# Half slabs of the memory keys and values inside the steps of the forgetting attention, and its forget sums added on VectorE

## The reference, cut to what matters

```python
rq, rk, rv, rg, fq, fk, fv, ff = split(rmsnorm(x, g_mix) @ w_in)        # 8 + 8 heads of 64
ret = silu(rg) * head_group_norm(chunk_retention(rotary(rq), rotary(rk), rv), g_ret_out)
F = cumsum(log_sigmoid(ff + b_forget))                                    # per head and token
logits = q.k / 8 + F[query] - F[key], causal                              # forgetting attention
h = x + concat([ret, softmax(logits) @ fv]) @ w_out
kv = rmsnorm(mem, g_mem) @ w_xkv                                          # 256 memory tokens
k, v = split(kv);  k = rmsnorm(k per head of 256, g_xk)
h = h + cross_attention(rmsnorm(h, g_xattn) @ w_xq, k, v) @ w_xo
h = h + (silu(hn @ w_gate) * (hn @ w_up)) @ w_down                        # then the second block
```

## Time and profile before

| | us |
|---|---|
| median of 3 runs | 1389.61 (1389.35 to 1390.12) |
| the profiled execution, as timed | 1390.99 |
| its span in the profile | 1389.2 |
| retention on PE | 179.9 to 200.6 |
| forgetting attention on PE, first to last step | 201.4 to 253.1 |
| first matmul of "out" | 306.5 |

### The profile page before, as it was taken

How to read it: one execution, slowest core, us unless ns; L and a number is a source line. 1 busy time by engine, 2 the same in 40 slices (tenths; PEclk the granted TensorE clock), 3 DMA queues, 4 the chain that set the end, 5 groups by cost and what they waited for, 6 DMA issues and landing times.

```text
span 1389.2 us, 17280 instructions
## 1 busy us (share of the span) xinstructions
PE 1354.4 (97%) x6530; PEld 1089.1 (78%) x6530; DVE 664.3 (48%) x978; ACT 623.5 (45%) x867; POOL 613.6 (44%) x448
## 2 busy tenths in 40 slices
PE   8999999999999999999999999988999999999999
PEld 7877955888876888888888887854878888888887
DVE  5434948355452553434343317588256455554111
ACT  5555238544364443433432123688244545554211
POOL 3444320474520455556555544312336555555453
PEclk9999999999999999999999999999999999999999
DMA  7223220152220244444346432200312222323422
GB/s 269 92 91 106 75 99 24 61 182 91 91 77 15 91 152 150 146 148 146 136 144 265 173 130 106 92 31 31 122 61 91 91 98 95 108 91 136 182 92 91
DMA packets 29216, 155.23 MB, mean 112 GB/s; under 512 B 3057, under 2 KB 4465, under 8 KB 14961
## 3 DMA queue, kind: packets, MB, share of 16 engines
q1 hardware_dynamic: 29168, 154.57, 31.1%
HBM read 152.46 MB, written 2.10 MB: 111 GB/s over the span
## 4 chain that ended last, share of the span: by engine, by line
issue 39%; PE 30%; POOL 26%; DVE 4%; DMA 1%; POOLq 0%; SPq 0%; ACT 0%
POOL wlo L392 26%; PE lin L1400 10%; PE lin L1402 10%; PE lin L1401 10%; DVE small L1045 1%; DVE expd L1056 1%; DMA raw<-w_slabs 1%; PE lin L1628 0%; DVE xl L899 0%; DVE win L1277 0%; DVE small L1049 0%; POOLq L401 0%; DVE xl L923 0%; DVE tmp L905 0%; PE att L1465 0%
## 5 line engine op out<-in xcount | busy, mean ns | idle before, releaser
L392 POOL TENSOR_TENSOR wlo<-raw,whi 128x512 fp32r<-128x512 f32 x444 | 613.4, 1414 | 760.2 <-ACT whi L419 501.1
L1400 PE MATMUL lin<-xh,whi 128*128 128x512 f32 x1072 | 420.5, 392 | 5.4 <-POOL wlo L392 3.6
L1402 PE MATMUL lin<-xh,wlo 128*128 128x512 f32 x1072 | 417.4, 389 | 0.0
L1401 PE MATMUL lin<-xl,whi 128*128 128x512 f32 x1072 | 417.2, 389 | 0.0
L1400 PEld LDWEIGHTS lin<-xh,whi 128*128 128x128 f32 x1072 | 201.2, 188 | 55.4 <-issue 9.0
L419 ACT ACTIVATE whi<-raw 128x2048 fp32r<-128x2048 f32 x66 | 126.7, 1919 | 261.8 <-PE lin L1402 256.2
L1402 PEld LDWEIGHTS lin<-xh,wlo 128*128 128x128 f32 x1072 | 201.2, 188 | 42.4
L1401 PEld LDWEIGHTS lin<-xl,whi 128*128 128x128 f32 x1072 | 201.3, 188 | 41.3 <-issue 0.2
L1400 PE MATMUL lin<-fh,whi 128*128 128x512 f32 x352 | 137.0, 389 | 0.0
L1401 PE MATMUL lin<-fl,whi 128*128 128x512 f32 x352 | 136.9, 389 | 0.0
L1402 PE MATMUL lin<-fh,wlo 128*128 128x512 f32 x352 | 136.9, 389 | 0.0
(11 more groups left out here) (337 smaller groups left out, 1919.7 us busy)
## 6 DMA issues: line engine op xcount, KB each, us to landing
raw<-w_slabs SPq DMA_DIRECT2D x111, 1024.0 KB, 4.8
adar<-ada SPq DMA_DIRECT2D x48, 512.0 KB, 5.5
decay<-decay SPq DMA_DIRECT2D x4, 512.0 KB, 7.9
h<-x_t SPq DMA_DIRECT2D x3, 512.0 KB, 6.5
out_t<-h SPq DMA_DIRECT2D x3, 512.0 KB, 8.2
rope<-rope SPq DMA_DIRECT2D x2, 512.0 KB, 7.2
memx<-mem_t SPq DMA_DIRECT2D x1, 1024.0 KB, 5.6
adar<-c_row SPq DMA_DIRECT2D x2, 512.0 KB, 6.1
```

The costliest lines, as they stand in the source:

```text
L392: return nc.gpsimd.tensor_tensor(wlo[s][:, ks, :], raw[s][:, ks, :], f(whi[s][:, ks, :]), ALU.subtract)
L1400: nc.tensor.matmul(out, whi_, xhi_, start=first, stop=False)
L1401: nc.tensor.matmul(out, whi_, xlo_, start=False, stop=False)
L1402: return nc.tensor.matmul(out, wlo_, xhi_, start=False, stop=last)
```

## The change

- PE puts one half slab of the memory (24 matmuls of 256 columns) behind the transposes of each of the 16 steps: slabs 14 to 21 are done in steps 0 to 15. The stage between the attention and "out" is gone. "out" starts with the slab form that waits for each input tile (first_pair).
- ACT, in every odd step, takes the result of the slab out of PSUM and then makes whi of the slab after next (memory_out). So whi of slab 22, the first of "out", is made in step 13, and that of slab 23 in step 15.
- PE no longer adds F by selr.fstack in each step. It makes these products once per head, 512 columns wide, in retention (forget_sums); ACT copies them to SBUF (minus_sums), and DVE adds the scores to them and takes the minimum of the negated sums in one instruction (tensor_tensor_reduce), which also writes the sums back to PSUM. The exponential then has scale -1.
- Memory norm (memx load, squares, sums, hi and lo) and the first parts of the group norm move into retention; the reciprocals and products of the group norm move into steps 1 to 13 on DVE.
- Retention's banks are dealt out differently: blocks s = 0 and s = 3 share two banks, and block s = 1 shares its two with the forget sums.
- SP: memx comes before the decay tables of pairs 2 and 3; the tile of w_ada comes after slabs 22 to 25. The row c still comes after the wait for all scores and ahead of slab 22.
- In slabs 4 to 7 ACT makes whi between the copies of the two tiles and not behind both.
- Two unused numbers in the count of bank pairs are gone, and some tiles lie elsewhere in SBUF.

```diff
@@ SyncE @@
             load_pairs(1, SLAB0["memk"] // 2 + 1)
+            sp.wait_ge(slab_done, SLAB0["memk"])
+            sp.dma_start(memx[:, :, :], mem_t.rearrange("(k p) m -> p k m", p=P)).then_inc(tables_in, 16)
             for c in range(2, RET_HEADS // 2):
...
-            sp.wait_ge(ret["pv"], RET_HEADS // 2)
-            sp.dma_start(memx[:, :, :], mem_t.rearrange("(k p) m -> p k m", p=P)).then_inc(tables_in, 16)
...
             load_pairs(SLAB0["memk"] // 2 + 1, SLAB0["out"] // 2)
             sp.wait_ge(fox["scores"], 32)
             load_c()
+            load_pairs(SLAB0["out"] // 2, SLAB0["xq"] // 2)
+            sp.wait_ge(xkn["out"], 2 * X_HEADS)
             load_ada(0, 0)
-            load_pairs(SLAB0["out"] // 2, SLAB0["ffn"] // 2 + 2)
+            load_pairs(SLAB0["xq"] // 2, SLAB0["ffn"] // 2 + 2)
@@ ScalarE @@
                     last.then_inc(rope["copy"], 1)
-                make_hi(u + 2)
+                    if j == 0:
+                        make_hi(u + 2)
...
+            def forget_tiles(c):
+                for hh in range(2):
+                    act.wait_ge(ff["mm"], 1 + 2 * c + hh + 1)
+                    nc.scalar.activation(minus_sums[c][hh][:, :], att[2 + hh], ACT.Copy).then_inc(ff["minus"], 1)
...
+            def memory_out(u):
+                g = SLAB0["memk"] + u
+                act.wait_ge(slab_done, g + 1)
+                if 2 <= u <= 4:
+
+                    act.wait_ge(xkn["stat"], (u - 1) if u < 4 else X_HEADS)
+                for j in range(2):
+                    b = lin[3][:, j * M:(j + 1) * M]
+                    if u < 4:
+                        nc.scalar.activation(kx_square[u % 2][:, j * M:(j + 1) * M], b, ACT.Square)
+                        last = nc.scalar.activation(kx[:, 2 * u + j, :], b, ACT.Copy, scale=pcol("g_xk", j))
+                    else:
+                        if u == 4 and j == 0:
+                            act.wait_ge(xkn["vscale"], 1)
+                        last = nc.scalar.activation(vx[:, j, (u - 4) * COLS:(u - 3) * COLS], b, ACT.Copy, scale=mem_scale[:, j:j + 1])
+                last.then_inc(pair_free, 1)
+                make_hi(g + 2)
+
             def beside_fox_act(j):
...
+                if j % 2 == 1 and j < 16:
+                    memory_out(j // 2)
+                if j in (3, 6, 9, 12):
+                    gn_hi(j // 3 - 1)
@@ VectorE, softmax_dve @@
-                            last = nc.vector.tensor_reduce(ring(j, "max")[:, e:e + 1], att[n % 4][:, 0:width(j)], AX.X,
-                                                           ALU.max, negate=True)
+                            row = att[n % 4][:, 0:width(j)]
+                            if added is None:
+                                last = nc.vector.tensor_reduce(ring(j, "max")[:, e:e + 1], row, AX.X, ALU.max, negate=True)
+                            else:
+                                last = nc.vector.tensor_tensor_reduce(row, row, added(n), -1.0, BIG, ALU.add, ALU.min,
+                                                                      ring(j, "max")[:, e:e + 1])
@@ TensorE, retention @@
-                        if n == 4:
+                        if s == 0 and i >= 1:
+
+                            pe.wait_ge(ret["mul"], n - 1)
+                        if s == 1 and i >= 1:
+                            pe.wait_ge(ff["minus"], 2 * (i - 1) + hh + 1)
...
+            pe.wait_ge(ff["sums"], 4)
+            retention_scores(0, range(TT))
+            forget_sums(0)
+            for i in range(1, 4):
+                retention_scores(i, range(3))
+                retention_values(i - 1)
+                retention_scores(i, [3])
+                forget_sums(i)
+                if i >= 2:
+                    gn_variance(i - 2)
+            memory_sums()
+            retention_values(3)
+            gn_variance(2)
@@ TensorE, forgetting attention @@
                 return [(bank[:, 0:w], qf[r:r + HEAD, c, P * t:P * (t + 1)], kf[r:r + HEAD, c, 0:w]),
-                        (bank[:, 0:w], selr[r:r + HEAD, P * hd:P * (hd + 1)], fstack[r:r + HEAD, 0:w]),
                         (bank[:, P * t:w], identr[:, :], maskr[:, :])]
...
             def beside_fox(j):
-                if j >= 16:
-                    first_keys(j - 16)
...
+                if j < 16:
+                    memory_part(j)
+                if j == 0:
+                    gn_variance(3)
```

More of the change, by code:

```diff
@@ L43 @@
 NEG = -1e30
+BIG = 3e38
 MODS = 6 * D // P
@@ L561, in _, with retained, memory_hi @@
+            def retained(c):
                 act.wait_ge(ret["pv"], c + 1)
                 nc.scalar.activation(heads_out(c), lin[c % 2][:, :], ACT.Copy).then_inc(ret["ev"], 1)
-            def softmax_act(a, steps, group, tbank, width, blocks, scaled, out, hi_out, extra=None, late=1):
+            def memory_hi(k):
+                nc.scalar.activation(memh[:, k, :], memx[:, k, :], ACT.Copy, scale=pcol("g_mem", k)).then_inc(norms["mem"]["hi"], 1)
+            forget_tiles(0)
+            act.wait_ge(tables_in, 3 * 16)
@@ new lines, in _ @@
+            for u in range(4):
+                nc.scalar.activation(tmp[u][:, :], memx[:, 2 * u:2 * u + 2, :], ACT.Square).then_inc(norms["mem"]["sq"], 1)
+            retained(0)
+            forget_tiles(1)
+            gn_square(0)
+            for k in range(4):
+                memory_hi(k)
+            retained(1)
+            forget_tiles(2)
+            gn_square(1)
+            gn_root(0)
+            for k in range(4, 8):
+                memory_hi(k)
+            retained(2)
+            forget_tiles(3)
@@ L568, in output, with softmax_act @@
+            gn_square(2)
+            gn_root(1)
+            act.wait_ge(norms["mem"]["sum"], 1)
+            nc.scalar.activation(mem_scale, lin[3][:, M:M + 2], ACT.Sqrt, bias=ccol(C_EPS)).then_inc(xkn["vsd"], 1)
+            retained(3)
+            gn_square(3)
+            gn_root(2)
+            gn_root(3)
+            def softmax_act(a, steps, group, tbank, width, blocks, scaled, out, hi_out, extra=None, late=1, sign=1.0):
                 def output(c):
@@ L626, in _ @@
[L626 to L651, removed]
+                nc.scalar.activation(foxh[:, c, :], lin[2][:, :], ACT.Copy).then_inc(fox["hi"], 1)
@@ L1651, in beside_fox @@
[L1651 to L1668 removed]
+                if c < 2:
+                    pe.wait_ge(xkn["var"], 2 * (c + 1))
@@ new lines, in fox_free, with memory_part @@
+                if c >= 1:
+                    pe.wait_ge(fox["lo"], c)
+            def memory_part(q):
+                u, half = q // 2, q % 2
+                g, p = SLAB0["memk"] + u, PAIR0["memk"] + u
+                if half == 0:
+                    pe.wait_ge(wlo_ready, g + 1)
+                    if u == 0:
+                        pe.wait_ge(xkn["vscale"], 1)
+                    else:
+                        pe.wait_ge(pair_free, p + 2)
+                out = lin[3][:, M * half:M * (half + 1)]
+                tile = slice(P * half, P * (half + 1))
+                for k in range(KT):
+                    if q == 0:
+                        pe.wait_ge(norms["mem"]["lo"], k + 1)
+                    if u < 4:
+                        mm = three(out, whi[u % 2][:, k, tile], wlo[u % 2][:, k, tile], memh[:, k, :], meml[:, k, :],
+                                   k == 0, k == KT - 1)
+                    else:
+                        mm = three(out, memh[:, k, tile], meml[:, k, tile], whi[u % 2][:, k, :], wlo[u % 2][:, k, :],
+                                   k == 0, k == KT - 1)
+                if half == 1:
+                    mm.then_inc(slab_done, 1)
@@ new lines, in key_squares, with between_fox @@
+            def key_squares(first):
+                for hd in range(first, first + 2):
+                    pe.wait_ge(pair_free, PAIR0["memk"] + hd + 3)
+                    for j in range(2):
+                        mm = nc.tensor.matmul(lin[2][:, M * (hd % 2):M * (hd % 2 + 1)], mean_d,
+                                              kx_square[hd % 2][:, j * M:(j + 1) * M], start=(j == 0), stop=(j == 1))
+                    mm.then_inc(xkn["stat"], 1)
+            def between_fox(j):
+                if j == 4:
+                    pe.wait_ge(ret["sd"], 4)
+                    key_squares(0)
+                if j == 8:
+                    pe.wait_ge(fox["lo"], 1)
+                    key_squares(2)
```

313 lines of the change are left out of this document (146 added, 167 removed).

## The result

| | us |
|---|---|
| before | 1389.48 (1387.95 to 1390.12) |
| after | 1395.98 (1390.97 to 1397.32) |
| ratio | 1.0046, 95% interval 1.0034 to 1.0059 |
| the profiled execution after | 1397.32, its span 1395.5 |

The change makes the kernel 0.46% slower, 6.5 us, where no change was forecast (1389.4; the upper end of the range, 1396.0, just holds it).

What follows compares the result with a forecast made beforehand. PE's work, idle gaps and slow clock were taken to bound the kernel. Terms -2.1, -7.4, -3.2, -4.3, +1.7, +0.7, +0.9 and +13.5 sum to -0.2 us: 1389.4 us on the median, range 1383 to 1396.

Steps and rivals of the forecast that it cites:

- the tail: End of the attention: PE stops for slab 22's late load, then whi of slab 23 and slow clock; +13.5 us, bounds 10 to 16.
- The F product in the steps: Attention steps: dropping F saves 0.43 us per pair at 512 columns, -4.3 us in all.
- The trace disagrees: F products: rejected the rule that different rows run together (0.2 us a pair), since the pair with F is 0.43 longer.
- +1.7 and +0.7: Retention: four pairs of forget sums at 0.43 us add 1.7; new waits for DVE's multiplication of block 3 add 0.7.
- whi between the copies: Slabs 4 to 7: whi comes 2.4 us earlier, so PE's gaps of 1.05 and 1.02 us go; -2.1 us.
- The gaps: PE's 7.8 us idle in the stretch of the change: all go but 0.4 us at retention's start; -7.4 us.
- The clock: PE's slow clock in the first steps and behind the 2.07 us gap goes with the gaps; -3.2 us.
- Rival 2: Steps: ACT sets the pace, PE standing 1.3 us at each of 8 slabs; +10 us, 1399; chance 0.10.
- Rival 1: End of the attention: slab 22 doesn't hold PE, or hardly; -10 us, 1379.6; chance 0.12.
- Rival 3: Retention comes out longer by +3 us and the clock falls anyway, +2 us; 1394.5; chance 0.18.
- The new reduction: DVE in the steps: some 0.7 us at 512 columns, bounds 0.6 and 1.2 per head, hidden by PE's half slab.
- the term for the cut slabs: Memory slabs cut in halves: one more switch each and breaks into other work, 8 x 0.1, +0.9 us; bounds 0 and 2.2.

Runs made afterwards that it cites:

- experiment 1: The changed kernel with SP issuing the loads of slabs 22 and 23 ahead of the wait for all scores and of c: 1384.33 us, ratio 0.9969 to before.
- experiment 2: The changed kernel with only whi of slab 23 made later, behind the last copies; slab 22 still late: 1391.49 us, ratio 1.0019 to before.
- experiment 3: The changed kernel (now version 3) with slabs 22 and 23 loaded before the scores wait and slab 23's whi behind the last copies: 1380.96 us, ratio 0.9938.
- experiment 4: The changed kernel plus 21 unused products of 256 columns on PE ahead of step 15's transposes, in the long gap: 1393.5 us, ratio 1.0038 to before.
- experiment 6: The kernel of experiment 3 with a 64-row pair of products, wide as the F product, put back into the steps: 1381.25 us, ratio 0.9941 to before.
- Experiment 7: The kernel of experiment 3 with the eight F products in retention 128 columns wide instead of 512: 1380.05 us, ratio 0.9936 to before.
- experiment 5: The kernel before, with only whi made between the two tiles' copies in slabs 4 to 7: 1385.4 us, ratio 0.9977 to before.
- experiment 8: The kernel of experiment 3 with the key squares' means behind step 4's half slab, not ahead of it: 1381.83 us, ratio 0.9943 to before.

## Why the prediction was right and wrong

**The mechanism of the tail was right, its size was not.** This term was 13.5 us with an upper bound of 16, and measured 17.9. Of that 12.56 is idle, where the forecast had 8.6 + 2.2 + 0.7 = 11.5. The first gap was 0.7 longer, most of it because slab 22 had landed only by 293.27, 6.6 us behind the end of the scores, instead of 6.1; slab 23 was on the way beside it, which the forecast didn't count. The other 5.33 is lower clock, where the forecast had 1.2 + 0.8. **This is the step that failed**: I took the length of a slow stretch behind a gap of 8.6 us from one behind a gap of 2.07 us (3.3 us) and put only 2.4 us of work into it. With the long gap the clock was already low for 4.7 us of the gap and stayed low for 5.7 us of work. I also charged half of 1.6 us for the second gap, and 2.85 came. That is 1.1 + 3.3 = 4.4 us too little, of the 6.6 by which the median was missed. Experiments 1 to 4 carry this: from mask to "out" 13.3 us go without the late load, 4.2 without the second whi, 16.6 without both.

**The F product in the steps was mis-sized: -4.3 in the sum, -2.3 measured.** I subtracted a form with 64-row pairs on both sides (0.86 us) from one with 128-row products on both sides (1.29). The same place without F is in the trace of after:

```profile
218.18 1.13 PE L1676 MATMUL c_act<-kf,qf 64*128 64x512 f32 x4
219.24 0.44 PE L1676 MATMUL c_act<-maskr,identr 128*128 128x128 f32 x2
```

1.06 us and not 0.86, so F cost 0.23 of the 1.29. The other 0.2 belongs to the neighbours and is still paid: the same form takes 0.96 in retention of after with a 128-row product ahead and a 64-row pair behind (193.88 to 194.84), so about 0.1 at either side. At the widths 128, 256 and 384 the distances from scores to mask shrink from before to after by 0.06 (0.49 to 0.43), 0.12 (0.75 to 0.63) and 0.17 us (1.02 to 0.85). That makes 0.58 per group of four steps, 2.3 in all, and experiment 6 agrees with 0.22 at the widest. The sentence "The trace disagrees" was therefore wrong: the rule weighed there (the Trainium skill, TensorE: Matmul & The Clock Gate, Part 3: Packing small matmuls), that products on different rows of the array run together, makes the pair cost one product, 0.2 us by the working there, and the rows show 0.23 here.

**In retention it did not hold so plainly.** There a pair of sums takes 0.62 (186.73 to 187.35), 0.60 (192.23 to 192.83) and 0.40 us (198.57 to 198.97), against the 0.43 I took and the 0.2 of the rule. Experiment 7 shows that this is not the sums' own price: waits for DVE take their place. With the first pair (1.32 us with its wait of 0.37) the four distances make 2.9 us, where +1.7 and +0.7 stood. The steps gave back 2.3. So moving F to retention seems to have bought nothing; no run keeps the new banks and leaves the sums out, so this isn't shown. Retention as a whole took 27.6 us where "about 27" stood.

**Right.** whi between the copies: -2.1 forecast, retention started 2.45 us earlier, and experiment 5 measured 3.2 (1.9 to 4.4). The gaps: none left in the steps but 1.05 at step 4 and 0.37 in retention, where 0.4 was kept. The clock: 1.00 through all steps. That the 3.2 us for it came back is in part luck: experiment 5 shows an execution with the same gaps and nothing lost, and how much of the miss on the medians lies there stays open. Rival 2 is out: ACT's passes kept up with PE in all odd steps but one. Rival 1, that slab 22 doesn't hold PE, is out by experiment 1. Rival 3's time (1394.5) is near the measured one, but not its mechanism: retention was no 3 us longer and the clock fell only in the tail. The new reduction takes 0.69 us and 0.14 for its accumulator read, as estimated from 1215 ns at twice the width. In the term for the cut slabs 8 x 0.1 is 0.8 and not 0.9.

**The wait nobody named** stands in step 4: 1.05 us until ACT has taken slab 15 out. I had weighed ACT's work over two steps as a mean. What counted was its place in one step, behind a reduction that DVE makes only after its group norm products, and experiment 8 shows that moving PE's work around it doesn't help.

**The account.** "out" was forecast to start at about 306.3 (306.49 less 0.2) and started at 312.04: 5.7 us. The tail makes 4.4 of it, the steps 1.2 (F by 2.0 and the wait by 1.05, less some 1.9 by which the rest came cheaper than its terms; cutting the slabs can be 0.9 of that at most) and the start of the steps 0.2. The steps' smaller terms were not measured apart. Behind "out" the span grew by another 0.7 us. Between 330 and 450 us the clock reads 0.97 in after and in experiments 1, 3 and 8, but 0.99 in before and in the other experiments. The long gap stands in 2 with 0.99, and 6 and 7 share the tail of version 3 and have 0.99. So it goes neither with the long gap nor with the second whi and may be scatter between executions; the cause stays open.

## What to carry to other kernels

Before work is moved earlier on one engine, ask at what point the transfer that feeds it is issued, and behind which wait: the transfer must move by as much, or the in-order engine stops for it and takes everything queued behind it along. What an instruction costs is read between the same neighbours: take the distance of two starts from a place with the same predecessor and successor, not from one that merely has the same form. And a gap on TensorE is priced with the slow work behind it: here, in the profiled execution, 12.6 us of gaps cost 5.3 us more, and closing 1.8 us of a gap gave 4.6. Such a price is one of an execution: the same gap of 2.07 us cost clock in before and none in experiment 5.

## What the runs showed of the hardware

- Slow work behind a gap was 5.7 us behind that of 9.33 in after, and 3.3 us behind one of 2.07 in before; behind the same 2.07 in experiment 5 the clock held. Behind gaps of 0.75 and 0.74 it held (experiments 2 and 3), behind 2.54 and 0.69 or 0.74 (after, experiment 1), or 0.80, 1.45 and 0.74 (experiment 4), it fell.
- In the half slab behind the gap, products of 256 columns that start every 0.12 us at the upper level (2.4 GHz) started every 0.21 us at the lower; the last product of the attention took 4.34 us instead of 2.37.
- Two 64-row products of 512 columns between another 64-row pair and a 128-row product add 0.22 to 0.23 us. The q.k pair of that width takes 0.86 us between 64-row pairs, 0.96 behind a 128-row product and 1.06 between two of them.
- c, slab 22 and slab 23, 2.5 MB issued within 1.2 us: c landed 3.4 us after its issue, slab 22 5.9 us after its own and 6.6 after that of c, slab 23 7.8 us after its own. In before, slab 21 and c took 6.05 us from the first issue, also with a third transfer behind them.
